# One context product moved into the first feed-forward block's last down product

## The reference

```python
x = x + 0.5 * m_x[2] * swiglu(modulate(rmsnorm(x, norm_g[l, 0]), m_x[0], m_x[1]), ffn1_w1[l], ffn1_w2[l])
ctx = ctx + 0.5 * m_c[2] * swiglu(modulate(rmsnorm(ctx, norm_g[l, 0]), m_c[0], m_c[1]), ffn1_w1[l], ffn1_w2[l])
px = modulate(rmsnorm(x, norm_g[l, 1]), m_x[3], m_x[4]) @ w_in[l]
pc = modulate(rmsnorm(ctx, norm_g[l, 1]), m_c[3], m_c[4]) @ w_in[l]
qx, kx, vx, gx, ux, vgx = split_proj(px)
qc, kc, vc, gc, uc, vgc = split_proj(pc)
...
x = x + m_x[5] * (jnp.concatenate([ret_x, gm_x], axis=-1) @ w_out[l])
x = x + 0.5 * m_x[8] * swiglu(modulate(rmsnorm(x, norm_g[l, 2]), m_x[6], m_x[7]), ffn2_w1[l], ffn2_w2[l])
return rmsnorm(x, final_g)
```

## Time and profile before

| what | value |
|---|---|
| median of 3 runs | 2152.24 us |
| lowest, highest | 2151.6, 2157.2 us |
| the profiled execution | 2157.13 us |
| its span | 2155.3 us |
| PE busy, share of the span | 2089.4 us, 97% |
| DVE, ACT, POOL busy | 72%, 32%, 35% |
| mean granted clock of TensorE | 0.987 |

### The profile page before, as it was taken

How to read it: one execution, slowest core, us unless ns; L and a number is a source line. 1 busy time by engine, 2 the same in 40 slices (tenths; PEclk the granted TensorE clock), 3 DMA queues, 4 the chain that set the end, 5 groups by cost and what they waited for, 6 DMA issues and landing times.

```text
span 2155.3 us, 28755 instructions
## 1 busy us (share of the span) xinstructions
PE 2089.4 (97%) x10408; PEld 1746.5 (81%) x10408; DVE 1559.8 (72%) x2198; ACT 680.3 (32%) x1063; POOL 747.2 (35%) x452
## 2 busy tenths in 40 slices
PE   8999989999999999989999999798999999999997
PEld 4999978888888888877989898677888888888886
DVE  4987687777777777687354468799777777777767
ACT  4234433322232323255212212245332223222322
POOL 1000044434343434345222222465434344343431
PEclk9999999999999999999999999999999999999998
DMA  7964311110111111132010333430111111101112
GB/s 298 360 244 156 128 49 59 58 58 30 58 58 58 45 42 58 59 105 97 20 40 21 127 102 131 139 108 10 59 59 49 39 58 58 58 31 57 58 40 78
DMA packets 37465, 181.35 MB, mean 84 GB/s; under 512 B 4368, under 2 KB 5648, under 8 KB 23184
## 3 DMA queue, kind: packets, MB, share of 16 engines
q1 hardware_dynamic: 32784, 163.57, 20.7%
q10 hardware_dynamic: 4608, 16.78, 2.4%
HBM read 175.09 MB, written 5.24 MB: 84 GB/s over the span
## 4 chain that ended last, share of the span: by engine, by line
PE 86%; DVE 9%; ACT 2%; issue 2%; POOL 1%; DMA 0%; SPq 0%; ACTq 0%; DVEq 0%
PE PS L1876 14%; PE PS L1878 14%; PE PS L1877 14%; PE PS L2036 12%; PE PS L2037 12%; PE PS L2038 12%; PE PS L1979 4%; DVE X L1497 1%; DVE ACC L1201 1%; DVE AS L1339 1%; PE PS L1934 1%; PE PS L2233 1%; PE PS L1912 1%; DVE AS L1318 0%; DMA AW<-ada_units 0%
## 5 line engine op out<-in xcount | busy, mean ns | idle before, releaser
L1497 DVE SCALAR_TENSOR_TENSOR X<-PS,GATE,X 128x512 f32<-128x512 f32 x704 | 484.5, 745 | 185.6 <-PE PS L1878 185.5
L658 POOL TENSOR_TENSOR WVL<-WR,WVH 128x512 fp32r<-128x512 f32 x168 | 238.3, 1429 | 564.7 <-ACT WVH L869 563.9
L1876 PE MATMUL PS<-PXH,W2H 128*128 128x512 f32 x672 | 266.5, 397 | 10.1 <-DVE X L1497 10.1
L2036 PE MATMUL PS<-HH,WVH 128*128 128x512 f32 x672 | 265.4, 395 | 0.0
L1878 PE MATMUL PS<-PXH,W2L 128*128 128x512 f32 x672 | 265.3, 395 | 0.0
L2037 PE MATMUL PS<-HL,WVH 128*128 128x512 f32 x672 | 264.7, 394 | 0.0
L2038 PE MATMUL PS<-HH,WVL 128*128 128x512 f32 x672 | 264.0, 393 | 0.0
L1877 PE MATMUL PS<-PXL,W2H 128*128 128x512 f32 x672 | 263.4, 392 | 0.0
L658 POOL TENSOR_TENSOR WVL<-ST,WVH 128x512 fp32r<-128x512 f32 x125 | 185.8, 1486 | 80.7 <-ACT WVH L869 80.1
L1876 PE MATMUL PS<-HH,WH 128*128 128x512 f32 x416 | 168.0, 404 | 16.6 <-POOL WL L632 11.8
L1878 PE MATMUL PS<-HH,WL 128*128 128x512 f32 x416 | 164.0, 394 | 0.0
(11 more groups left out here) (258 smaller groups left out, 4404.8 us busy)
## 6 DMA issues: line engine op xcount, KB each, us to landing
WR<-w_units SPq DMA_DIRECT2D x89, 1024.0 KB, 5.4
W2R<-w_units SPq DMA_DIRECT2D x44, 512.0 KB, 3.5
AW<-w_units ACTq DMA_DIRECT2D x32, 512.0 KB, 4.2
AW<-ada_units SPq DMA_DIRECT2D x11, 1024.0 KB, 13.9
W2RB<-w_units SPq DMA_DIRECT2D x22, 512.0 KB, 3.6
AW<-w_units SPq DMA_DIRECT2D x8, 1024.0 KB, 6.6
X<-x SPq DMA_DIRECT2D x2, 2048.0 KB, 9.8
out<-OUT SPq DMA_DIRECT2D x2, 1024.0 KB, 4.2
```

Of the source, the lines that this page charges most:

```text
L658: pool.tensor_tensor(WVL[:, slot], src, WVH[:, slot].bitcast(F32), ALU.subtract).then_inc(s_wl, 1)
L1497: dve.scalar_tensor_tensor(xv, y_bank(n)[:, :], GATE[:, 2 * f, d, 0:1], xv, ALU.mult, ALU.add).then_inc(s_fyd, 1)
L1876: pe.matmul(dst, wh, xh, start=first, stop=False)
L2036: pe.matmul(bank[:, :], wh, xh, start=first, stop=False, skip_group_check=True)
```

## The change

The context keys' first product (n = 0) leaves the list and stands between the two halves of the last down product (`context_product`). For this ACT modulates the context tokens inside the last period, between the two last gate copies (`context_modulated`), and GpSimd makes HCL ahead of the low part of unit 0. The norm of latents' block 1 starts between the halves: VectorE adds its squares after the 8 downs of t = 0 and makes mean and diagonal among those of t = 1; TensorE makes its row sums after the second product of t = 1, its scale after the last. The squares of block 2 are added among the scalings of block 1 and TensorE's sums of them stand after n = 2 instead of n = 1. Unit 2's low part goes from VectorE to GpSimd, between the power of block 1 and the low parts of its tiles.

```diff
@@ gpsimd
             feed_forward(0)
-            for t in range(2):
-                pool.wait_ge(BS[0].fl[t], NF)
-            low(0)
             pool.wait_ge(BS[0].m[5], NF)
             for k in range(KT):
                 pool.wait_ge(s_hh, 8 * J[1, 0] + k + 1)
                 pool.tensor_tensor(HCL[:, k, :], XC[:, k, :], HCH[:, k, :].bitcast(F32), ALU.subtract).then_inc(s_hl, 1)
+            for t in range(2):
+                pool.wait_ge(BS[0].fl[t], NF)
+            low(0)
             low(1)
             norm_rsqrt(1, 1)
+            low(2)
+            norm_low(1, 1, 0, 6)
             norm_rsqrt(1, 2)
-            norm_low(1, 1)
+            norm_low(1, 1, 6, KT)
             norm_low(1, 2)
@@ scalar
+                def context_modulated():
+                    act.wait_ge(s_spill, 32)
+                    act.wait_ge(s_coef, 6)
+                    for k in range(KT):
+                        act.activation(XC[:, k, :], XC[:, k, :], ACT.Identity, scale=GAIN[:, 1, k, 1:2],
+                                       bias=MODS[:, 3 * KT + k, 1:2]).then_inc(s_hf, 1)
+                        act.wait_ge(s_hf, 8 * J[1, 0] + k + 1)
+                        act.activation(HCH[:, k, :], XC[:, k, :], ACT.Copy).then_inc(s_hh, 1)
...
                         act.activation(LAST[t][0], src.rearrange("p (k c) -> p k c", k=4), ACT.Copy).then_inc(s_fh[t], 1)
+                        if f == 0 and t == 0:
+                            context_modulated()
...
-            for k in range(KT):
-                if k == 4:
-                    mix_high(2)
+            mix_high(2)
+            def second_square(k):
                 act.wait_ge(BS[0].fyd, NYB + 16 * (NF - 1) + KT + k + 1)
                 square(1, 2, k)
-            mix_high(3)
+            for k in range(4):
+                second_square(k)
             for b in (1, 2):
                 for k in range(KT):
...
                     norm_high(1, b, k, k + 1)
+                    if b == 1 and k == 2:
+                        mix_high(3)
+                        for m in range(4, KT):
+                            second_square(m)
@@ vector
                 for t in range(2):
+                    if f == 0 and t:
+                        add_squares(1, 1)
                     for k in range(KT):
                         down(NF - 1, t, k)
+                        if f == 0 and t and k == 1:
+                            norm_mean(1, 1)
+                        if f == 0 and t and k == 4:
+                            norm_diagonal(1, 1)
@@ tensor
                 down(NF - 1, 0, last=True)
-                down(NF - 1, 1, last_norm if f else lambda d: None, last=True)
+                if f == 0:
+                    context_product(0)
+                down(NF - 1, 1, last_norm if f else first_norm, last=True)
             feed_forward(0)
-            for n, (i, name, a, b) in enumerate(FILLS):
+            norm_scale(1, 1)
+            for n, (i, name, a, b) in enumerate(FILLS[1:], 1):
...
-                if n == 0:
-                    norm_sum(1, 1)
-                if n == 1:
-                    norm_scale(1, 1)
+                if n == 2:
                     norm_sum(1, 2)
                 if n == 3:
                     norm_scale(1, 2)
```

More of the change, by code:

```diff
@@ L1051, in _ @@
             high(0, 16 * unit_count(0))
-            act.wait_ge(s_spill, 32)
-            act.wait_ge(s_coef, 6)
-            for k in range(KT):
[L1055 to L1059, removed]
             act.wait_ge(BS[0].fy, 16 * (NF - 1))
@@ L1661, in context_keys @@
                 ins.then_inc(s_free[n], 1)
[L1663 to L1672, removed]
             dve.wait_ge(s_hl, 8 * (J[1, 0] + 1))
@@ L1676, in _ @@
                 scaled(1, 1, k)
-                if k == 1:
-                    norm_mean(1, 2)
-                if k == 2:
+                if k == 3:
+                    for m in range(4):
+                        add_square(1, 2, m)
+                if k == 5:
                     unit_low(3)
-                if k == 3:
-                    norm_diagonal(1, 2)
+                    for m in range(4, KT):
+                        add_square(1, 2, m)
+            norm_mean(1, 2)
+            norm_diagonal(1, 2)
             context_keys(0)
@@ L2009, in square_sum, with context_product, first_norm @@
                 return ins
+            def context_product(n):
+                slot = n % 2
+                wh, wl = WH[:, slot], WL[:, slot]
+                pe.wait_ge(s_lo[slot], unit_count(n))
+                pe.wait_ge(s_hl, 8 * (J[1, 0] + 1))
+                for tb in range(2):
+                    for k in range(KT):
+                        t = slice(tb * P, (tb + 1) * P)
+                        ins = mm3(PS[n][:, tb * UC:(tb + 1) * UC], HCH[:, k, t], HCL[:, k, t],
+                                  wh[:, k, :], wl[:, k, :], k == 0, k == KT - 1)
+                ins.then_inc(s_fill, 1)
+            def first_norm(d):
+                if d == 1:
+                    norm_sum(1, 1)
             def last_norm(d):
@@ L2183, in _ @@
                 if name in ("ck", "cv"):
-                    pe.wait_ge(s_hl, 8 * (J[1, 0] + 1))
                     for tb in range(2):
```

## The result

| what | before | changed |
|---|---|---|
| median | 2154.16 us (5 runs) | 2164.63 us (5 runs) |
| lowest, highest | 2151.6, 2157.2 | 2162.92, 2166.89 |
| profiled execution, its span | 2157.13, 2155.3 us | 2166.89, 2165.1 us |
| mean granted clock | 0.987 | 0.985 |
| ACT's first gate copy to the first latent keys | 57.7 us | 66.1 us |

The change makes the kernel slower: 1.0047 of the time before, 95% interval 1.0037 to 1.0058, some 10 us. The forecast was 2160.7, that is 8.5 us or 0.4% over the 2152.24 it started from.

The account below looks back on a forecast made before the run. TensorE, busy 97% of the span, was taken as the bound, so only its waits count. Second norm's sums 12.1 us later, less 3.6 given back, made +8.5 us: 2160.7 from 2152.24, range 2150 to 2168.

Parts of the forecast that it names:

- Part 4: Second norm's additions meet GpSimd's tile low parts; its sums start at 977.7, 12.1 us later, after TensorE waits 7 us.
- Part 1: Context tokens between ACT's last gate copies: 0.93 us a pair, second gate copy at 933.5, +1.5 us.
- Part 2: Context product inside the last down: first norm's additions done 3.8 us earlier, TensorE's gap 3.3 us instead of 4.46.
- Part 3: Block 1's diagonal held to 958.5 by GpSimd's unit 2 low part; first scale 5.2 us earlier, 2.5 lost.
- unit loaded at about 966.0: Unit 3's weights land then, ACT's high part ends at 967.9, VectorE's low part runs 969.5 to 971.8.
- if the additions were not held up at all, +1.8: Lower bound for the second norm: last four additions done at 973.2, scale at 979.8, loss only 1.8 us.
- The clock behind the second wait: After the 7 us wait the clock is low: 1.73 us for the sums, about 7.0 for the fourth product.
- Everything behind it keeps its distances: Behind the first latent keys nothing gives a shift back, so their +8.5 us carries to the end.
- C: Rival: product fills the gap at 950, sums follow without wait, clock stays full; -7.7 us, 2144.5; chance 0.10.
- B: Rival: block 2's additions slip between GpSimd's low parts; +1.8 us, 2154; chance 0.15.
- E: Rival: unit 4's load slower or clock low after the 3.3 and 2.5 us gaps too; +10 or more; chance 0.10.
- D: Rival: GpSimd holds up only the copy, not two-input additions or the diagonal; -1 us, 2151; chance 0.05.

Follow-up runs that it names:

- e1: Changed kernel with block 2's squares added in one piece behind the last down and GpSimd's second power ahead of the tiles, as before; ratio 1.0008 to before, keys +58.4.
- e2: Kernel before with only block 2's additions moved among block 1's scalings and their row sums behind n = 2; ratio 1.0063 to before, keys +71.6.
- e3: Changed kernel with GpSimd's low part of unit 2 waiting for VectorE's diagonal of block 1; ratio 1.0040 to before, keys +68.0.
- e4: Changed kernel with GpSimd's low parts of block 1's eight tiles cut to 32 of 512 columns; ratio 1.0029 to before, keys +64.3.
- e12: Changed kernel with unit 3's load ahead of the constants' load, GpSimd's tiles at full length; ratio 1.0049 to before, keys +66.9.
- e6: Changed kernel with GpSimd's block 1 tiles cut to 32 columns and unit 3's load ahead of the constants'; ratio 1.0010 to before, keys +59.4.
- e7: Changed kernel with 40 filler matmuls between the third context product and the second norm's sums; ratio 1.0047 to before, keys +67.1.
- e9: Version with retuned engine orders and earlier weight loads, here with the second norm's scale behind the fourth context product; ratio 0.9987 to before, keys +52.3.

## Why the prediction was right, and where it was off

The sign, the size (8.5 us forecast up to the keys, 8.4 measured) and the place are right, and e1 and e2 show that it is Part 4. That the sum came within 0.1 us is in part luck: several of its terms were off by 1 to 2.4 us and made up for each other.

- Part 1 held: second gate copy forecast at +8.0 (933.5), measured +8.1; pairs 0.94 apart.
- Part 2 held in its waits: copy 3.48 (3.3 forecast, 942.1 to 945.4), TensorE idle 3.12 (3.3). It missed the clock, which I let stay high behind that gap: it fell to 0.55, and the first scale came at +34.1 instead of +33.0.
- Part 3 was mis-sized: the diagonal was held 0.9 us (1.63 less 0.69) and not 3.0 (3.7 less 0.7), since the downs ahead of it came late at the low clock, when GpSimd was nearly through with its low part. e3 shows that even these 0.9 were hidden by TensorE's own products, so "2.5 of it lost here" is wrong.
- Part 4, the term that decides: sums forecast at +52.3, measured +51.9, idle 7 forecast, 5.48 measured, as TensorE's products ahead of the wait ended 1.2 later than forecast. The first four of them took what I had given them (copy 1.46, three additions 4.09, forecast 1.4 and 4.1), and e4 shows that it is GpSimd's tiles that hold them up. The last four took 4.83, not 6.0, and began 0.7 us late: unit 3's high part came 2.4 us later than "unit loaded at about 966.0" has it, because SyncE's queue puts that load behind the constants' and the constants' behind the last down. The two errors belong together and made up for each other: with the load in time (e12) the last four took 5.90, as forecast, and the sums began at +52.6. So the bound "if the additions were not held up at all, +1.8" was wrong as it stood: that kernel measured +6.6 (e4), and +1.7 only with the load moved as well (e6). The mistake was to follow the queues that steps are moved past, but not the one that waits for the last down: the change moved that, and with it unit 3's load from +23.5 to +36.0.
- The clock behind the second wait: from the sums to the scale 9.0 us, 8.7 forecast. e6, where it stayed high behind a wait of 1.68, needed 6.7; that fillers could have saved it is not shown, as e7 failed.
- "Everything behind it keeps its distances" held up to block 2's keys (8.4 us later too), but 2.2 us more came at the end of the program, an effect that other orders of the kernel have as well and whose cause is open.
- Rivals. C needed the second sums before 971.3, which is +45.8; they came at +51.9. B needed small hold-ups; the copy's and the additions' were as forecast. E happened in part. The low clock behind the first gap came, and the first scale a microsecond later than forecast; what that cost the keys no run isolates. The late load of unit 4 came too (ACT waited 4.13 us for it and ended its high part at 985.63), still ahead of VectorE's low part at 988.02; in e7 it was late enough to cost 1 us. D falls by e4: the same two-input additions took 0.78 each without the tiles beside them and 1.36 with them. The Trainium skill's two passages that the prediction names (Advanced Engine Details and Errata, VectorE Performance Modes; VectorE: DVE Perf Modes, Why `tensor_tensor` can't do 2×_2P or 4×) speak of two-port modes alone, which such an addition does not have. But the first of these pages of the Trainium skill, Advanced Engine Details and Errata, says under GPSIMD Details that VectorE's instructions with two SBUF inputs conflict with GpSimd as well. These runs agree with that (1.36 against 0.78), so the prediction's "by that alone the sum would be D's" came from an incomplete reading and not from a difference between page and trace.

## What to carry to other kernels

A product moved forward fills one gap and uncovers another: count, for each wait, how many products are left behind it. An addition of VectorE among GpSimd's tiles cost 1.4 us here instead of 0.8, so it belongs where GpSimd is idle. And when an edit moves an instruction that a queue waits for, follow every load behind that wait: its price shows only once the wait ahead of it is gone. Measure at more than one landmark: e9 gained 1.9 us at the first keys and lost 0.6 two products later.

## What the runs showed of the hardware

- A VectorE instruction on two SBUF tiles, or a copy of one, that met a GpSimd instruction ended 0.3 to 0.6 us behind it: the copy of block 1 took 3.48 instead of 0.42 and ended 0.28 behind GpSimd's low part, the diagonal took 1.63 instead of 0.68 and ended 0.55 behind. With GpSimd's tiles shortened (0.25 to 0.5 us each) block 2's copy took 0.42 instead of 1.46, and three of its additions 0.78 each instead of 1.36. It goes the other way too: a GpSimd tile of 1.3 us took 2.96, from 988.50 on, beside VectorE's low part of unit 4 in the changed kernel.
- The granted clock fell to 1.2 GHz behind TensorE's waits of 2.91, 3.12 and 5.48 us, and stayed at 2.4 GHz behind one of 1.68. Behind 3.12 it was not the same each time: e1's sums took 1.05 us where the changed kernel's took 1.44. In e7, with fillers at full clock and then 1.93 us of wait, the sums were still at 2.4 GHz, but over 5 us from their start the clock was 0.66.
